# Moving work between engines at the start, the joins and the attention of a two-layer backbone kernel

## The reference

```python
for layer in range(2):
    sh, sc, gt = split(silu(c) @ w_mod + b_mod)            # once for c, once for c_ctx
    h = rms_norm(x, g_pre) * (1 + sc) + sh                 # latent and context tokens
    if layer == 0:
        u, g, f, gf = split(h @ w_in)                      # 4 x 1024 columns
        u = conv4(u); r = rglru_both_directions(u)         # gates from 64x64 blocks, two scans
        y = concat([r * silu(g), (real(fft2(f)) @ w_f + b_f) * silu(gf)]) @ w_out
    else:
        q, k, v, g = split(h @ w_in)                       # 16 query heads, 4 kv heads
        y = window_attention(rope(q), rope(k), v, sink) * silu(g) @ w_out
    x = x + gt * rms_norm(y, g_post)
```

## Time and profile before

| | |
|---|---|
| median of 3 runs | 1547.27 us (1544.95 to 1547.94) |
| the profiled execution: its own time, its span | 1549.56 us, 1547.8 us |
| PE busy, DVE, ACT, POOL, share of the span | 90%, 55%, 47%, 38% |
| mean granted TensorE clock | 0.96 of 2.4 GHz |

### The profile page before, as it was taken

How to read it: one execution, slowest core, us unless ns; L and a number is a source line. 1 busy time by engine, 2 the same in 40 slices (tenths; PEclk the granted TensorE clock), 3 DMA queues, 4 the chain that set the end, 5 groups by cost and what they waited for, 6 DMA issues and landing times. The chain is left out here.

```text
span 1547.8 us, 20035 instructions
## 1 busy us (share of the span) xinstructions
PE 1390.6 (90%) x7152; PEld 1160.6 (75%) x7152; DVE 854.9 (55%) x1217; ACT 730.4 (47%) x1147; POOL 586.6 (38%) x274
## 2 busy tenths in 40 slices
PE   3879999999999999848999976999996999998897
PEld 2658788888888888737888855778885888887676
DVE  6885768686767768642111124122221788888532
ACT  5364646383737464542212213222221888887511
POOL 1322323323232223244434414334442566665642
PEclk9889999999999999979999987999998899999999
DMA  9312121312222212074343425624335533240684
GB/s 385 119 68 94 55 94 54 106 45 103 71 81 68 88 60 75 0 254 162 109 136 95 119 96 181 166 92 132 97 110 140 175 118 103 75 143 29 183 232 128
DMA packets 95284, 179.61 MB, mean 116 GB/s; under 512 B 10464, under 2 KB 57344, under 8 KB 92928
## 3 DMA queue, kind: packets, MB, share of 16 engines
q1 hardware_dynamic: 95232, 178.93, 35.9%
HBM read 123.84 MB, written 45.11 MB: 109 GB/s over the span
## 5 line engine op out<-in xcount | busy, mean ns | idle before, releaser
L832 PE MATMUL slab<-h_hi,w_hi 128*128 128x512 f32 x720 | 258.5, 359 | 7.3 <-DVE h_lo L279 7.3
L834 PE MATMUL slab<-h_hi,w_lo 128*128 128x512 f32 x720 | 257.7, 358 | 0.0
L833 PE MATMUL slab<-h_lo,w_hi 128*128 128x512 f32 x720 | 257.5, 358 | 0.0
L797 POOL TENSOR_TENSOR w_lo<-wraw,w_hi 128x1024 fp32r<-128x1024 f32 x31 | 78.7, 2539 | 341.2 <-ACT w_hi L507 341.2
L1827 POOL TENSOR_TENSOR probs<-probs,rdenom 128x2560 f32<-128x2560 f32 (+1 forms) x32 | 136.6, 4269 | 59.8 <-DVE rdenom L1784 59.8
L832 PEld LDWEIGHTS slab<-h_hi,w_hi 128*128 128x128 f32 x720 | 135.8, 189 | 29.8 <-DVE h_lo L279 7.5
L1506 PE MATMUL slab<-h_hi,w_hi 128*128 128x512 f32 (+1 forms) x352 | 136.7, 388 | 17.8 <-DVE h_lo L1428 17.0
L833 PEld LDWEIGHTS slab<-h_lo,w_hi 128*128 128x128 f32 x720 | 135.8, 189 | 22.2
L834 PEld LDWEIGHTS slab<-h_hi,w_lo 128*128 128x128 f32 x720 | 135.7, 188 | 22.2
L1236 PE MATMUL Y<-wo_hi,m_hi 128*128 128x512 f32 x320 | 128.2, 401 | 23.2 <-DVE wo_lo L1151 20.9
L1507 PE MATMUL slab<-h_lo,w_hi 128*128 128x512 f32 (+1 forms) x352 | 136.0, 386 | 0.0
(11 more groups left out here) (275 smaller groups left out, 3038.3 us busy)
## 6 DMA issues: line engine op xcount, KB each, us to landing
wraw<-in_w_in SPq DMA_DIRECT2D x32, 512.0 KB, 3.4
wm<-in_wm SPq DMA_DIRECT2D x32, 512.0 KB, 3.5
mixT<-work SPq DMA_DIRECT2D x16, 640.0 KB, 3.7
mraw<-mixT SPq DMA_DIRECT2D x20, 512.0 KB, 5.2
wm<-in_wm SPq DMA_DIRECT2D x8, 1024.0 KB, 15.2
q_parts<-qT SPq DMA_DIRECT2D x32, 256.0 KB, 4.8
oT<-o_out SPq DMA_DIRECT2D x8, 1024.0 KB, 3.9
work<-in_xT SPq DMA_DIRECT2D x8, 640.0 KB, 8.1
```

What stands on the lines that cost most here:

```text
L832: nc.tensor.matmul(out, l_hi, r_hi, start=start, stop=False)
L833: nc.tensor.matmul(out, l_hi, r_lo, start=False, stop=False)
L834: return nc.tensor.matmul(out, l_lo, r_hi, start=False, stop=stop)
```

## The change

Setup: DVE does `split_lo` of the first three slabs (two between the last `add_square` and the root, one at k = 4) and silu of the conditioning rows, in one operation each (at k = 6 and 7); POOL does neither. PE runs 6 matmuls of the identity with itself after each of the squares 4 to 8. The tables go to `H` and `sgf`, after `h_lo` 5. First round: all of GF comes before the gate products of direction 0, G chunks 0 and 1 between the two directions, G chunk 2 after the DFT product; silu of GF is made chunk by chunk, and `y_lo` is made by DVE. All rounds: silu of G goes to `fT`, and the copy of the cosine part to `B`. Attention: `TB` has three banks, `O` one; `copy_o` stands right after the copy of the next unit's tile 0, with the factor 0.5; POOL does the first mixing, in two parts in block 6.

```diff
@@ setup, ACT, DVE, PE
+            if k == 4:
+                act.wait_ge(hl, 4)
+                split_hi(2)
...
-        act.wait_ge(hl, 10)
-        split_hi(2)
...
         for k in range(1, KT):
             add_square(k)
+        split_lo(0)
+        split_lo(1)
...
             h_low(k - 1)
+            if k == 4:
+                split_lo(2)
+            elif k >= 6:
+                silu_rows(k - 6)
...
+        for k in range(3, KT):
+            pe.wait_ge(sqd, k + 1)
+            for i in range(6):
+                nc.tensor.matmul(W4[:, 0:P], ident[:], ident[:], start=True, stop=True)
@@ mixers
-        tab_pieces = [(A[:, 0:half], slice(0, half)), (B[:, 0:half], slice(half, TAB_N))]
+        tab_pieces = [(H[:, 0:half], slice(0, half)), (sgf[:, 0:half], slice(half, TAB_N))]
...
-            sp.wait_ge(hl, 4)
+            sp.wait_ge(hl, 10)
@@ ACT, a round
-                if not first:
-                    act.wait_ge(yd, t)
+                if first:
+                    split_hi(t, SLAB_G)
+                else:
+                    act.wait_ge(mr, t)
                     f_rows(t, False)
...
+                if first:
+                    silu_gf(t, True)
                 gates(t, 0, first)
...
                 root(t, 0)
+                if first:
+                    tanh_g(t, (0, 1))
+                else:
+                    silu_gf(t, False)
                 gates(t, 1, first)
...
                 root(t, 1)
+                tanh_g(t, (2,) if first else range(3))
+                act.wait_ge(uv, t + 1)
                 act.wait_ge(hd, 2 * t + 2)
-                for c, (at, n) in enumerate(CHUNKS):
-                    act.wait_ge(s_g, 3 * t + c + 1)
-                    nc.scalar.activation(B[:, at:at + n], slab[:, c, 0:n], ACT.Tanh, scale=0.5).then_inc(tg, 1)
-                act.wait_ge(uv, t + 1)
-                nc.scalar.activation(fT[:, 0:UV_N], Wf[:, 0:UV_N], ACT.Identity,
+                nc.scalar.activation(B[:, 0:UV_N], Wf[:, 0:UV_N], ACT.Identity,
@@ DVE, a round
+                    silu_gf(0)                              # first round, after the tables
...
+                if first:
+                    silu_gf(1)
+                    silu_gf(2)
                 direction(0)
+                if first:
+                    dve.wait_ge(yh, 1)
+                    tt(y_lo, xf[:], v32(y_hi), ALU.subtract).then_inc(yl, 1)
                 scan(0)
+                if first:
+                    silu_g(0)
+                    silu_g(1)
...
@@ PE, a round
-                    slab_product(t, SLAB_GF, True, (1,))
+                    slab_product(t, SLAB_GF, True, (1, 2))
...
                 gate_products(t, 0)
-                slab_product(t, SLAB_GF, first, (2,) if first else range(3))
+                if first:
+                    slab_product(t, SLAB_G, True, (0, 1))
+                else:
+                    slab_product(t, SLAB_GF, False)
                 gate_products(t, 1)
                 dft_product(t)
-                slab_product(t, SLAB_G, first)
+                slab_product(t, SLAB_G, first, (2,) if first else range(3))
@@ attention: ACT, POOL, PE
-                        if x == 1:
+                        if x == 0:
                             if u:
                                 copy_o(b, s, u - 1)
...
+                    if is_block(b, NB - 2) and u == 1:
+                        first_sum()
+                    elif is_block(b, NB - 2) and u == 2:
+                        first_mixed()
...
-                if x == 0 and not (is_block(b, 0) and u < 2):
-                    pe.wait_ge(oe, 4 * b + u - 1)
+                if x == 0 and not (is_block(b, 0) and u == 0):
+                    pe.wait_ge(oe, 4 * b + u)
```

More of the change, by code:

```diff
@@ L555, in f_tokens, with silu_gf, tanh_g @@
                     nc.scalar.activation(xf[:, at:at + n], W[:, c, 0:n], ACT.Copy).then_inc(xr, 1)
+            def silu_gf(t, first):
+                if first:
+                    act.wait_ge(tab_l, 2)
+                else:
+                    act.wait_ge(mf, t)
+                for c, (at, n) in enumerate(CHUNKS):
+                    act.wait_ge(s_gf, 3 * t + c + 1)
+                    nc.scalar.activation(sgf[:, at:at + n], slab[:, c, 0:n], ACT.Tanh, scale=0.5).then_inc(tgf, 1)
+            def tanh_g(t, chunks):
+                for c in chunks:
+                    at, n = CHUNKS[c]
+                    act.wait_ge(s_g, 3 * t + c + 1)
+                    nc.scalar.activation(fT[:, at:at + n], slab[:, c, 0:n], ACT.Tanh, scale=0.5).then_inc(tg, 1)
             def table_hi(i):
@@ L634, in _, with split_lo, silu_rows @@
         def _(dve):
-            set_vector(dve)
+            def split_lo(j):
+                dve.wait_ge(wh[j % 2], j // 2 + 1)
+                hi, lo = (buf[:, j % 2].rearrange("p k n -> p (k n)") for buf in (w_hi, w_lo))
+                if j == SLAB_GF:
+                    hi, lo = gf_hi[:, 0:D], gf_lo[:, 0:D]
+                nc.vector.tensor_tensor(lo, wraw[:, j % 2, :], v32(hi), ALU.subtract).then_inc(wl[j % 2], 1)
+            def silu_rows(w):
+                dve.wait_ge(thb, w + 1)
+                nc.vector.scalar_tensor_tensor(out=silu_b[:, w, :], in0=wm1[:, w, :], scalar=1.0, in1=silu_b[:, w, :],
+                                               op0=ALU.add, op1=ALU.mult).then_inc(sbd, 1)
+            set_vector(dve, split_lo, silu_rows)
             def mod_sums(t, q):
@@ L646, in body, with silu_gf, silu_g @@
             def body(t, first, last):
+                stt = nc.vector.scalar_tensor_tensor
+                def silu_gf(c):
+                    at, n = CHUNKS[c]
+                    dve.wait_ge(tgf, 3 * t + c + 1)
+                    stt(out=sgf[:, at:at + n], in0=sgf[:, at:at + n], scalar=1.0, in1=slab[:, c, 0:n],
+                        op0=ALU.add, op1=ALU.mult).then_inc(sgfd, 1)
+                def silu_g(c):
+                    at, n = CHUNKS[c]
+                    dve.wait_ge(tg, 3 * t + c + 1)
+                    stt(out=fT[:, at:at + n], in0=fT[:, at:at + n], scalar=1.0, in1=slab[:, c, 0:n],
+                        op0=ALU.add, op1=ALU.mult).then_inc(sg, 1)
                 if not first:
@@ L753, in body @@
                 scan(1)
-                for c, (at, n) in enumerate(CHUNKS):
-                    dve.wait_ge(tg, 3 * t + c + 1)
-                    stt(out=B[:, at:at + n], in0=B[:, at:at + n], scalar=1.0, in1=slab[:, c, 0:n],
-                        op0=ALU.add, op1=ALU.mult).then_inc(sg, 1)
+                for c in (2,) if first else range(3):
+                    silu_g(c)
                 dve.wait_ge(us, t + 1)
@@ L807, in body @@
                 split_lo(t, SLAB_G)
-                pool.wait_ge(yh, t + 1)
-                sub(y_lo, xf[:], v32(y_hi), ALU.subtract).then_inc(yl, 1)
+                if not first:
+                    pool.wait_ge(yh, t + 1)
+                    sub(y_lo, xf[:], v32(y_hi), ALU.subtract).then_inc(yl, 1)
                 if not last:
@@ L813, in body @@
                 sub(H[:], H[:], E[:, 0:T], ALU.add).then_inc(hs, 1)
-            split_lo(0, SLAB_U, True)
-            split_lo(0, SLAB_F, True)
-            for w in range(2):
-                pool.wait_ge(thb, w + 1)
-                sub(wm1[:, w, :], wm1[:, w, :], silu_b[:, w, :], ALU.mult).then_inc(thp, 1)
-                pool.wait_ge(thp, w + 1)
-                sub(silu_b[:, w, :], wm1[:, w, :], silu_b[:, w, :], ALU.add).then_inc(sbd, 1)
             pool.wait_ge(modk, KT)
```

108 lines of the change are left out of this document (55 added, 53 removed).

## The result

The changed kernel takes 1519.83 us in the median of 4 runs (1519.47 to 1520.55), the kernel before beside it 1546.11 us (4 runs, 1542.05 to 1547.94). The ratio is 0.9834, with a 95% interval of 0.9813 to 0.9855: 26 us faster, 22 to 29 by the interval. The forecast was 1524.0 us in a range of 1511 to 1537.

What follows compares the result with a forecast made beforehand. PE fills the middle rounds, so gains lie in setup, first round and attention: 4.4 + 5.9 + 7.4 + 0 + 3.0 - 0.5 + 3.1 = 23.3 us, giving a median of 1524.0 us, range 1511 to 1537 (forecast case 1517 to 1530).

Steps and rivals of the forecast that it cites:

- Setup, warm start: Setup: identity products bring PE to its upper clock level, so its sums take half their length; 4.4 us gained.
- Setup, POOL's work to DVE: Setup: DVE's slow pairs beside POOL and PE's 5.34 us wait at the fifth product go; net 5.9 us gained.
- First round: First round of layer 0: reordered PE work cuts the 11.1 us tanh wait; 58.15 to 50.7 us, gain 7.4, bounds 3 and 11.
- Middle rounds: Later rounds of layer 0: the buffer exchange gains 0, bounds -2 and +2 us over all rounds.
- Attention units: Attention ring of PE, ACT and DVE: earlier copy_o gains 0.13 us a unit, 3 us over 24; third TB bank nothing.
- Last block: Last attention block, units without scores: PE comes sooner to the wait for the single O bank's copy; 0.5 us lost.
- Join: Join after block 6: mixing moved from DVE to POOL gains 6.5, gives 3.4 back; net 3.1 us, bounds 0 and 6.5.
- A: Setup rival: TensorE not warm in time, the sets delay the sums by 4.8 us; 1533 us, chance 0.15.
- B: First-round rival: no gain, as DVE bounds the chain at butterflies and scan; 1531 us, chance 0.16 shared with E.
- D: Attention rival: the single O bank becomes the bound; 1554 us, chance 0.04 with other losses of that size.
- E: Attention rival: units and join together gain nothing (5.6 us); 1530 us, chance 0.16 shared with B.
- C: Rival of more gain: PE at upper level from the start, ring 0.35 us a unit, join's upper bound; 1514 us, chance 0.13.

Runs made afterwards that it cites:

- no_identity: Changed kernel without the 5 sets of 6 identity products that keep PE busy in the setup; 1524.38 us, ratio to before 0.9863.
- pool_setup: Changed kernel with the first three slab splits and silu of the conditioning rows back on POOL; 1524.25 us, ratio to before 0.9872.
- g_late: Changed kernel with all of G behind the DFT product in the first round, as before; 1530.50 us, ratio to before 0.9896.
- silu_g_in_B: Changed kernel with the old buffers for silu of G and the cosine copy in rounds 2 to 8; 1520.31 us, ratio to before 0.983.
- units_old: Changed kernel with two banks each of TB and O and the late copy out of O, as before; 1524.26 us, ratio to before 0.9868.
- combined: Changed kernel with `kept_busy` and `pool_pieces` edits, two banks each of TB and O, late copy in block 7; 1513.34 us, ratio to before 0.9786.
- pool_pieces: Changed kernel with POOL's first mixing in four 128x512 pieces, one per unit of block 6; 1516.68 us, ratio to before 0.9808.
- mix_on_dve: Changed kernel with the first mixing back on DVE at the end of block 6; 1521.77 us, ratio to before 0.9852.
- kept_busy: Changed kernel with 4 identity products per set, sums 128 columns wide, wide identity products in PE's later setup waits; 1519.53 us, ratio to before 0.9824.

## Why the prediction was right

The time lies in the forecast case's own range. By its steps:

- **Setup, warm start: 4.4 forecast; the step that failed.** Its times were right (upper level at 19.1, sums 2.29 us), but the sums started 1.4 us late, and its chain was not right. The step took the level once reached as kept. It fell back twice: at 25.9 us without any wait of PE since 13.4, behind 20 records of 2 columns, and at 36.1 us in the 1.61 us wait ahead of the first slab product. The trace of the kernel before has this second fall too, and the forecast did not look there. So 1.4 us were left at the first slab product and none at the second (44.76 against 44.66). Taking the identity products out costs 1.1 us at GF and 0.7 at the end of layer 0 (`no_identity`); in the two profiles where only the second fall came and the rest is alike, layer 0 ends 2.0 to 2.6 us earlier still.
- **Setup, POOL's work to DVE: 5.9 forecast, 6.6 to 7.3 measured** (`pool_setup`; 4.9 without the warm start). The trace agrees with the rule that the forecast cited for it (the Trainium skill, *SBUF — State Buffer*, "SBUF: two separate sides"): pairs of 1.68 us take 4.19 and 5.85 beside POOL. In the first round the delay that the forecast feared from it did not come in full: one `mod_sums` takes 3.30 us beside POOL's split of G, but the other 1.41 in place of 3.97, as DVE waited for ACT until POOL's `u_lo` was nearly done.
- **First round: 7.4 forecast, 8.8 measured.** The forecast waits were 1.1, 2.5, 1.1 and 2.0; they are 0.61, 1.46, 1.15 and 2.13. Without them 44.0 us are left, the forecast's 42.7 + 1.3. What was mis-sized is the wait for the scan's tanh (1.0 less) and for silu of GF (0.5 less). G's two chunks carry it all (`g_late`). In the profiles with the short setup the round takes 50.6 to 51.2 us, so 7.0 to 7.6 is as fair a number for the gain as 8.8.
- **Middle rounds: 0 forecast, 0 measured**, and shown by `silu_g_in_B`.
- **Attention units: 3.0 forecast for 24 units, 4.5 measured in 20.** The mechanism was right, the size not: the ring was followed with 0.13 us a unit, and gained 0.20, until PE had no wait left. The third bank gives nothing, as forecast.
- **Last block: 0.5 forecast as lost, 1.0 to 1.1 measured** (`units_old`, and `combined` against `pool_pieces`), and for another reason than the one given: not the single bank, but the copy's place.
- **Join: 3.1 forecast, 3.06 measured** (`mix_on_dve`). ACT's stall behind POOL's sum is 2.14 us, where 2.1 (2.4 less 0.3) was forecast.

Of the rivals, A (not warm in time) happened in part: the sums started 1.4 us late, not 4.8. B, D and E did not; C's idea of a clock that stays up is what `kept_busy` brought. For the join the forecast left open whether a gap of some 2.7 us brings the lower level. It was 2.52 us and the product behind it took 0.80, so the rule named there (*TensorE: Matmul & The Clock Gate*, "HAM oscillation — how this bites in real kernels", of the Trainium skill), that idle gaps bring the lower level, holds here, and the join gained the forecast 3.1 us all the same. In the setup the rule is not enough: at 25.9 us the level fell without any gap.

That the edited stretches came so near the total (22.7 against 23.3) is luck: a term far too large (4.4) and a loss too small (the last block) stood against gains too small in the first round, in the units and, taken beside the warm start, in POOL's work. The 26.3 us between the medians hold some chance of the untouched code as well.

## What to carry to other kernels

Keeping TensorE at work before its first large product pays only if the level is still there when that product starts. Here it was lost behind thin products and in a wait of 1.61 us, and it was kept where the thin products were made wide and the waits filled (`kept_busy`). So look at the granted clock of the stretches behind the filler, not only at the first. Small products can be made wide almost for nothing (20 records of 128 columns take 2.50 us, of 2 columns 2.29, both at the upper level). When one engine's order is changed, ask at each place whether the engine would have waited anyway: ACT's early copy is free where it waits for transposes, and costs where no other work stands in the unit. Work given to an engine with idle time goes into the gap where that engine waits, cut to the gap's length (1.28 us pieces in a gap of 1.8), not between two duties that others wait for.

## What the runs showed of the hardware

- The same setup code ended at 72.2 to 72.4 us in 3 profiles and at 75.5 to 76.5 in 5. In the 3 the pace of PE doubled at 16.8 to 17.1 us and the clock fell once; in the 5 it doubled at 18.4 to 19.6 us and the clock fell twice, the first time at 25 to 26 us while PE worked on thin products without a wait. A single profile of a start is no measure of it.
- In the wait of 1.61 us ahead of the first slab product the clock fell to 0.50 in all 12 profiles that have this wait, those of the kernel before among them; in the two in which wide products fill it (`kept_busy`, `combined`) the clock stayed up. In all 12 the few us ahead of the wait were thin work too (32 columns of the array, or records of 2 columns), so the wait alone is not shown to be enough.
- POOL's 128x512 pieces, two SBUF operands, beside DVE's operations of the attention, which read PSUM, cost the unit nothing (7.08 and 7.06 us against 7.09 and 7.07), where POOL's work beside DVE's pairs with only SBUF operands in the setup made 1.68 into 4.19 and 5.85.
- Untouched code (the output projection and the projections of layer 1) took 538 to 547 us over 14 profiles, a wider spread than most of the terms that this study was about. It goes with the clock: TensorE was at the lower level for 58.6 us of it in the shortest (`mix_on_dve`, 538.3) and for 73.6 in the longest but one (`pool_pieces`, 546.9), and a line through all 14 has 0.48 us for each such us, with single points up to 2.5 us off it. So compare the time at the lower level before a difference of a few us is given to an edit.
